# First loads, first modulation and x's split in one block; half of an output projection's operand split inside the attention; a context's sums shared out anew

## The reference, cut to what matters

```python
mod = (silu_c @ w_ada[l] + b_ada[l])[:, None, :]        # for x;   mod_c the same for the context
q, k, v, g_a, xb, b_g, c_g, g_b = split_cols(modulate(x, shift, scale) @ w_in, widths)
hc = modulate(xc, shift_c, scale_c)                     # through the same w_in
o_a = window_attention(q, k, v, kc, vc, sink)
o_b = b_g * short_conv(c_g * xb, conv_w)
y = jnp.concatenate([o_a * silu(g_a), o_b * silu(g_b)], axis=-1) @ w_out
x_new = layer_norm(DEEPNORM_ALPHA * x + gate * y, ln_g, ln_b)
```

## Time and profile before

| | us |
|---|---|
| median of three runs (2543.55 to 2545.18) | 2544.41 |
| the profiled execution | 2544.61 |
| its span, first to last instruction | 2542.8 |
| TensorE busy | 2305.4 (91%) |
| VectorE busy | 1462.5 (58%) |
| ScalarE busy | 1079.4 (42%) |
| GpSimd busy | 284.4 (11%) |
| mean granted TensorE clock, share of full | 0.954 |

### The profile page before, as it was taken

One profiled execution on the slowest core, in us unless ns is written; L12 is line 12 of the kernel. 1 busy time (PEld: TensorE's weight loads), 2 busy tenths in 40 slices (PEclk: granted clock), 3 DMA queues, 4 the chain that ended last, 5 costly groups with the idle time before them and its releaser, 6 DMA issues. The chain is left out here.

```text
span 2542.8 us, 35881 instructions
## 1 busy us (share of the span) xinstructions
PE 2305.4 (91%) x15162; PEld 1884.8 (74%) x15162; DVE 1462.5 (58%) x2187; ACT 1079.4 (42%) x1705; POOL 284.4 (11%) x156
## 2 busy tenths in 40 slices
PE   4999989789999969798889999998998889999996
PEld 2888766678888856576578888876776588888865
DVE  2233484648787773546677666345456677666354
ACT  2211373447658553334634334243335534333342
POOL 0100002513223210101011000011101010000011
PEclk7999899889999989899999999999999989999998
DMA  8111104311112112230022222312230012222311
GB/s 324 64 67 61 40 2 184 115 56 54 52 51 59 51 35 105 76 123 34 5 91 84 99 100 100 108 67 83 95 122 18 18 67 86 97 100 99 108 61 72
DMA packets 35104, 205.18 MB, mean 81 GB/s; under 512 B 3840, under 2 KB 5376, under 8 KB 14720
## 3 DMA queue, kind: packets, MB, share of 16 engines
q1 hardware_dynamic: 34944, 202.88, 22.8%
HBM read 200.77 MB, written 2.10 MB: 80 GB/s over the span
## 5 line engine op out<-in xcount | busy, mean ns | idle before, releaser
L309 PE MATMUL ps<-a_high,w_high 128*128 128x512 f32 (+1 forms) x1680 | 632.7, 377 | 35.5 <-DVE a_low L2405 22.7
L310 PE MATMUL ps<-a_low,w_high 128*128 128x512 f32 (+1 forms) x1680 | 621.8, 370 | 0.0
L311 PE MATMUL ps<-a_high,w_low 128*128 128x512 f32 (+1 forms) x1680 | 621.1, 370 | 0.0
L309 PEld LDWEIGHTS ps<-a_high,w_high 128*128 128x128 f32 x1680 | 320.8, 191 | 100.3 <-DVE w_low L2019 19.6
L2019 DVE TENSOR_TENSOR w_low<-raw_ring,w_high 128x2048 fp32r<-128x2048 f32 x102 | 233.8, 2292 | 270.6 <-ACT w_high L2013 265.9
L310 PEld LDWEIGHTS ps<-a_low,w_high 128*128 128x128 f32 x1680 | 321.4, 191 | 54.1 <-issue 2.5
L311 PEld LDWEIGHTS ps<-a_high,w_low 128*128 128x128 f32 x1680 | 321.2, 191 | 53.0
L2013 ACT ACTIVATE w_high<-raw_ring 128x2048 fp32r<-128x2048 f32 x102 | 195.2, 1914 | 367.0 <-PE ps L311 280.7
L309 PE MATMUL ps<-x_high,place_high 128*128 128x512 f32 (+1 forms) x720 | 261.5, 363 | 33.8 <-POOL x_low L325 25.4
L310 PE MATMUL ps<-x_low,place_high 128*128 128x512 f32 (+1 forms) x720 | 255.8, 355 | 0.0
L311 PE MATMUL ps<-x_high,place_low 128*128 128x512 f32 (+1 forms) x720 | 255.4, 355 | 0.0
(11 more groups left out here) (368 smaller groups left out, 3971.1 us busy)
## 6 DMA issues: line engine op xcount, KB each, us to landing
raw_ring<-w_dram SPq DMA_DIRECT2D x112, 1024.0 KB, 4.9
place_raw<-wc_dram SPq DMA_DIRECT2D x48, 512.0 KB, 3.6
ada_ring<-w_dram SPq DMA_DIRECT2D x12, 1024.0 KB, 17.0
arena<-w_dram SPq DMA_DIRECT2D x12, 1024.0 KB, 7.0
place_raw<-w_dram SPq DMA_DIRECT2D x11, 1024.0 KB, 4.9
ab_raw<-w_dram SPq DMA_DIRECT2D x10, 1024.0 KB, 5.0
x<-xT_dram SPq DMA_DIRECT2D x1, 2048.0 KB, 24.1
out_dram<-x SPq DMA_DIRECT2D x1, 2048.0 KB, 7.2
```

Of the source, the lines that this page charges most:

```text
L309: nc.tensor.matmul(out, wh, xh, start=start, stop=False)
L310: nc.tensor.matmul(out, wh, xl, start=False, stop=False)
L311: return nc.tensor.matmul(out, wl, xh, start=False, stop=stop)
```

## The change

- One block, `stage_start`, takes the place of the first three stages and of the split in `stage_ab_in`. The `w_ada` ring has 5 slots in the memory of later stages. SP's order is: 8 units, ab's unit 0, x and the context in four parts of two tiles each, 4 units, ab's unit 1. Once shift and scale are there (8 units), VectorE splits ab's unit 0, then modulates tile after tile and makes all lows; ScalarE makes the highs and then multiplies `X` by alpha, with the copies of rows 4 and 5 in between. The gate's part of the modulation is added at the block's end.
- `cb` is loaded in `stage_ab_in` and cast there at the third tile. GpSimd is no longer used for `SplitTiles`; VectorE makes all lows, in `stage_out1` too.
- In the attention, ScalarE makes the highs of tiles 4 to 7 of the output projection's operand before its first exponentials, and GpSimd their lows. `stage_mid` splits tiles 0 to 3 only, and its products go 4 to 7, 0 to 3.
- In the context's layer norm VectorE makes the last two of the seven adds of the sum, and adds the squares in pairs, so that four products take the place of eight. GpSimd makes its eight lows of x in a row. Of the context's modulation, ScalarE makes the even tiles and VectorE the odd ones.

```diff
-            def split_low(self, eng, which, k):
-                if k >= 0 and k % 2 == which:
-                    eng.wait_ge(self.S.rms_high, k + 1)
-                    (nc.vector if which else nc.gpsimd).tensor_tensor(
-                        self.low[k], self.src[k], self.high[k].bitcast(f32), O.subtract)\
-                        .then_inc(self.S.rms_odd if which else self.S.rms_even, 1)
+            def split_low(self, dve, k):
+                dve.wait_ge(self.S.rms_high, k + 1)
+                nc.vector.tensor_tensor(self.low[k], self.src[k], self.high[k].bitcast(f32), O.subtract)\
+                    .then_inc(self.S.operand, 1)
...
+        raw_cb = arena1[:, ab_mark:ab_mark + NCB]
...
+        def stage_start():
...
+            chunks = [slice(2 * i, 2 * i + 2) for i in range(4)]
+            tiles_in = SplitTiles(S, [yin[:, k, :] for k in range(KT)], xh, xl)
+            with nc.Block() as block:
+                @block.sync
+                def _(sp):
+                    def unit(u):
+                        if u >= 5:
+                            sp.wait_ge(S.used, u - 4)
+                        sp.dma_start(ring[u % 5], d["w1"][U0["ada0"] + u]).then_inc(arrived[u % 5], 16)
+                    sp.sem_clear(N.range)
+                    sp.sem_clear(w_range)
+                    sp.dma_start(v1[:, :], d["v1"]).then_inc(S.load, 16)
+                    sp.dma_start(cf[:, :], d["cf"]).then_inc(S.load2, 16)
+                    for u in range(8):
+                        unit(u)
+                    ab_stream.fetch(sp, src_ab, 0)
+                    for i, ks in enumerate(chunks):
+                        sp.dma_start(X[:, ks, 0:L], d["xT"][:, ks, :]).then_inc(x_arrived[i], 16)
+                        sp.dma_start(X[:, ks, L:T], d["ctxT"][:, ks, :]).then_inc(x_arrived[i], 16)
+                    for u in range(8, 12):
+                        unit(u)
+                    ab_stream.fetch(sp, src_ab, 1)
+                    sp.wait_ge(S.load, 16)
+                    sp.wait_ge(S.load2, 16)
+                @block.tensor
+                def _(pe):
+                    def flip(b):
+                        pe.wait_ge(S.act_out, b + 1)
+                        for j in range(4):
+                            last = nc.tensor.matmul(PS[:, 6 + b // 4, 8 * b + 2 * j:8 * b + 2 * j + 2],
+                                                    rows[b % 2][:, j * P:(j + 1) * P], picks_, start=True, stop=True)
+                        last.then_inc(S.flipped, 1)
+                    for u in range(12):
+                        pe.wait_ge(arrived[u % 5], 16 * (u // 5 + 1))
+                        if u == 0:
+                            pe.wait_ge(S.act_step, 1)
+                        w = ring[u % 5].rearrange("p (k n) -> p k n", k=KT)
+                        for k in range(KT):
+                            g = slice(32 * (k % 4), 32 * (k % 4) + 32)
+                            last = nc.tensor.matmul(PS[g, u // 2, (u % 2) * 256:(u % 2 + 1) * 256],
+                                                    cond_[:, k, :], w[:, k, :], start=(k < 4), stop=(k >= 4))
+                        last.then_inc(S.used, 1)
+                        if u == 2:
+                            pe.wait_ge(S.ready, 2)
+                        if u % 2 == 0 and 2 <= u < 8:
+                            flip(u // 2 - 1)
+                        if u == 7:
+                            flip(3)
+                    flip(4)
+                    flip(5)
+                @block.scalar
+                def _(act):
+                    def turn(b):
+                        act.wait_ge(S.used, 2 * b + 2)
+                        if b >= 2:
+                            act.wait_ge(S.flipped, b - 1)
+                        nc.scalar.activation(rows[b % 2], PS[:, b, :], A.Copy).then_inc(S.act_out, 1)
+                    act.wait_ge(S.load, 16)
+                    act.wait_ge(S.ready, 1)
+                    nc.scalar.activation(cond_[:, :, 0:2], v1[:, 0:16].rearrange("p (w k) -> p k w", w=2), A.Silu)\
+                        .then_inc(S.act_step, 1)
+                    for b in range(4):
+                        turn(b)
+                    ab_stream.split_high(act, 0)
+                    for k in range(KT):
+                        act.wait_ge(S.dve_out, 2 * k + 2)
+                        tiles_in.split_high(act, k)
+                        if k == 5:
+                            turn(4)
+                    for k in range(KT):
+                        nc.scalar.mul(X[:, k, :], X[:, k, :], ALPHA)
+                        if k == 3:
+                            turn(5)
+                @block.vector
...
+                    def modulation(parts, bank, b):
+                        v = slice(16 * parts[0], 16 * parts[-1] + 16)
+                        bias = v1[:, V1["b_ada0"][0] + 8 * parts[0]:V1["b_ada0"][0] + 8 * parts[-1] + 8]
+                        dve.wait_ge(S.flipped, b)
+                        link(nc.vector.tensor_tensor(mod[:, v].rearrange("p (j w) -> p j w", w=2),
+                                                     PS[:, bank, v].rearrange("p (j w) -> p j w", w=2),
+                                                     bias.unsqueeze(2).to_broadcast([P, 8 * len(parts), 2]), O.add))
+                    nc.vector.memset(padded_, 0.0).then_inc(S.ready, 1)
+                    dve.wait_ge(S.load2, 16)
+                    nc.vector.tensor_reduce(picks_, ident.rearrange("p (g x) -> p x g", g=4)[:, 0:2, :], AX, O.add)\
+                        .then_inc(S.ready, 1)
+                    dve.wait_ge(S.load, 16)
+                    modulation((0, 1), 6, 4)
+                    link(nc.vector.tensor_scalar(mod[:, 16:32], mod[:, 16:32], 1.0, None, O.add))
+                    ab_stream.split_low(dve, 0)
+                    for k in range(KT + 1):
+                        if k < KT:
+                            if k % 2 == 0:
+                                dve.wait_ge(x_arrived[k // 2], 32)
+                            for who, (a, b) in enumerate(((0, L), (L, T))):
+                                nc.vector.tensor_scalar(yin[:, k, a:b], X[:, k, a:b], modv(0, 1, who, k),
+                                                        modv(0, 0, who, k), O.mult, O.add).then_inc(S.dve_out, 1)
+                        if k:
+                            tiles_in.split_low(dve, k - 1)
+                    modulation((2,), 7, 6)
...
                     sp.sem_clear(N.range)
+                    ab_stream.load(sp, src_ab, RAW, RAW + 1)
                     sp.dma_start(ca, d["ca"]).then_inc(S.load, 16)
                     sp.dma_start(nsink, d["sink"]).then_inc(S.load, 16)
-                    ab_stream.load(sp, src_ab, RAW, 13 + RAW + 1)
+                    sp.dma_start(raw_cb, d["cb"]).then_inc(S.load2, 16)
+                    ab_stream.load(sp, src_ab, RAW + 1, 13 + RAW + 1)
                     sp.wait_ge(S.load, 32)
...
-                    ab_stream.split_high(act, u0)
-                    tiles_in.on_act(act)
...
-                    ab_stream.split_low(dve, u0)
-                    tiles_in.on_dve(dve)
-                    dve.wait_ge(S.load, 32)
                     for i, (kind, j) in enumerate(tiles):
                         if weight_tile.get((kind, j), 1) % 2 == 0:
                             ab_stream.split_low(dve, u0 + weight_tile[(kind, j)] // 2 + 1)
+                        if i == 2:
+                            dve.wait_ge(S.load2, 16)
+                            link(nc.vector.tensor_copy(cb[:, :], raw_cb))
+                            dve.wait_ge(S.load, 32)
...
+                    for k in range(NT4, KT):
+                        nc.scalar.activation(xh[k], yin[:, k, :], A.Copy).then_inc(S.rms_high, 1)
...
+                @block.gpsimd
+                def _(pool):
+                    for k in range(NT4, KT):
+                        pool.wait_ge(S.rms_high, k - NT4 + 1)
+                        nc.gpsimd.tensor_tensor(xl[k], yin[:, k, :], xh[k].bitcast(f32), O.subtract)
...
-            tiles_in = SplitTiles(S, [yin[:, k, :] for k in range(KT)], xh, xl)
+            tiles_in = SplitTiles(S, [yin[:, k, :] for k in range(NT4)], xh, xl)
+            ORDER = [4, 5, 6, 7, 0, 1, 2, 3]
...
                         gather(1, k)
                     pool.wait_ge(S.pe_tile, KT)
-                    for k in range(4):
-                        low(0, k)
-                    for k in range(6, KT):
-                        gather(1, k)
-                    for k in range(4, KT):
+                    for k in range(KT):
                         low(0, k)
                     for n in range(2):
...
-                            if i == 0:
+                        for k in ORDER:
+                            if i == 0 and k < NT4:
                                 tiles_in.tile(pe, k)
                             last = product3(bank(i), wh[:, k, :], wl[:, k, :], xh[k][:, ts], xl[k][:, ts],
```

(56 more changed lines are left out.)

176 lines of the change are left out of this document (28 added, 148 removed).

## The result

The changed kernel took 2530.05 us, median of five runs (2526.62 to 2535.06), against 2543.55 (2542.57 to 2545.18, five runs) for the kernel before on the same chip: ratio 0.9942, 95% interval 0.9931 to 0.9953, or 13.5 us less. The prediction was 2526.4 with a range of 2519.5 to 2533, so it holds, with the median 3.6 us above the point. A second set of five runs, on another chip, gave 2528.05 against 2543.37; the median of all ten runs is 2529.05.

The account below looks back on a forecast made before the run. TensorE is busy for 91% of the span, so time is won only where it waits or runs at half clock. 11.4 - 1.9 + 6.3 + 1.6 + 0.6 = 18.0 off 2544.6, less 0.2: 2526.4 us; range 2519.5 to 2533.

Parts of the forecast that it names:

- The start: First block up to the first tile's end: TensorE starts at 53.8, tile ends at 61.1 against 72.51, 11.4 us won.
- The attention: Highs and lows added ahead of the first exponentials: these come 1.45 late, 1.9 us lost if VectorE's first shift is caught.
- the two cases that the prediction drew from that page: Attention, VectorE beside GpSimd's lows: held by the port, 1.9 us lost; or no contention with one SBUF input, 1.45.
- The output projection's first tile: Products go 4 to 7, then 0 to 3, without a wait: ends at 396.9 against 403.15, 6.3 us won.
- The context's sums: Context's layer norm: mean at 485.5 instead of 488.6, root 1.0 earlier, later stretch 0.6 shorter; together 1.6 us won.
- the chain of four adds of squares: Context's norm: four VectorE adds, each behind a GpSimd low of 1.24, the fourth behind a unit split of 2.33; done 496.8.
- the modulation's chain: Context's norm after the reciprocal: VectorE's 20 short steps become 16, four of them on ScalarE; stretch 0.6 us shorter.
- The second output projection: All eight lows on VectorE, the first ready at about 955.5 rather than 956.1: 0.6 us won.
- (1): Context's sums: GpSimd gets no turn between VectorE's adds; gain there 6.5 instead of 1.6, total 2521.5; chance 0.16.
- (2): Attention pays for each low on VectorE, 5.0 instead of 1.9, and start's paths come 2 us late: 2531.5; chance 0.19.
- (3): First projection stays at half clock, 4.8 us more a tile, so the change is slower: 2555 at six tiles; chance 0.03.
- (4): Gain is absorbed because weight loads paced the first stages: about 2544; chance 0.04, with the change doing less than said.

Follow-up runs that it names:

- mod_again: Changed kernel with the context's modulation as before (VectorE modulates all eight tiles, ScalarE makes only highs), measured a second time: 2528.15 us, ratio 0.9942.
- start_alone: Kernel before with only the new first block (loads, first modulation, x's split): 2534.01 us, ratio 0.9963.
- attn_undone: Changed kernel with all eight tiles split in the output projection, none in the attention, lows on VectorE: 2528.68 us, ratio 0.9939.
- number 4: The experiment with attn_undone: changed kernel without the attention's splits, 2528.68 us, ratio 0.9939.
- Number 6: Changed kernel with the context's modulation as before, all eight tiles on VectorE, measured twice: 2527.24 us (ratio 0.9935) and 2528.15 us (0.9942).
- number 2: The experiment with start_alone: kernel before with only the new first block, 2534.01 us, ratio 0.9963.
- numbers 7 and 8: Changed kernel with GpSimd's eight lows waiting for the context's sum (2531.08 us, ratio 0.9953), or for the sums of squares (2536.21 us, 0.9963).
- after_again: The changed kernel measured again without any edit, against the kernel before: 2528.05 us, ratio 0.9943.

## Why the prediction was right, point by point

**The start: right, 12.3 won for 11.4.** First product at 53.4 for 53.8, tile done at 60.24 for 61.1; ScalarE ended at 53.07 and the gate's add behind the flips at 51.57 in this profile, at 54.20 and 53.41 in mod_again: within one to two microseconds of each other, the forecast having 53.5 and 53.2. Of the 0.9 left over, half is the earlier start and half that six products and not nine ran cold. The other nine profiles with this start had the tile done at 60.3 to 62.2, so 11.4 lies in the middle of them.

**The attention: the head right, the last 0.4 by luck.** The delay at the head was 1.53 for 1.45. The forecast made 1.9 of it by a VectorE step caught on the path, and that step failed. VectorE was caught, in an add of 128x12 that took 1.52 and ended at 292.53, where GpSimd's third low ended (292.50), and in the second unit's shift of 0.60, which ended with the second low; the first shift took 0.25 for 0.17. But ScalarE was behind with its highs and its table load until 290.58, so the catches held nothing: in VectorE's maxima of the 24 units (24, not the 20 given ahead), the changed kernel ran 1.5 behind the one before from the fifth to the twenty-second. The other 0.4 came in the last two, and there start_alone and attn_undone, which have no split in the attention, lost 0.4 as well. Against those two the splits cost 2.0 in this profile. Against the kernel before, the nine profiles with the splits lost 1.1 to 1.9 where the end ran at full clock and 3.1 to 3.5 where half clock fell on it (number 4). The Trainium skill's page "SBUF — State Buffer" (Who interferes with whom) gives the port to whichever started first, for its whole instruction; the add of two SBUF inputs agrees. Of the two cases that the prediction drew from that page for a step with one SBUF input, the 0.60 against 0.17 is the held one. Reductions that read PSUM took 1.21 and 1.22, as before (1.23), caught by nothing.

**The output projection's first tile: right, 6.33 for 6.3.** It starts at 380.89, without a wait for an operand and at full clock. Number 4 shares it out: 2.9 from VectorE making every low, 3.4 from the four operands that lie ready. Against the attention's loss the second is a gain of 1.5 to 2.3, as long as no half-clock stretch takes it.

**The context's sums: right sign, both terms mis-sized, and much of the gain hangs on the clock.** The mean came 3.5 earlier for 3.1. The root came 4.3 earlier for 1.0: the step that failed is the chain of four adds of squares, of which I put the first behind a low and the fourth behind a unit split of 2.33. The first add took 0.44 with no wait; the other three took 1.48 to 1.49, each one low, 1.41 apart and not 1.66, and the last of GpSimd's eight lows (10.81 in all, to 476.16) was the one that the fourth met. The other failed step is the modulation's chain, 0.6 won by forecast and 1.8 lost in fact (14.54 from the reciprocal to the next layer for 12.76). Counting VectorE's steps was wrong: three of its four lows now wait 0.62 for a high, and ScalarE has a modulation and two highs in each pair. Number 6 takes 1.0 of it back; the rest is the norms' 1.88 for 1.1, the first of them held by GpSimd's unit splits that run to 480.96. The sum, 3.53 + 0.76 - 1.78 = 2.5, lay above the 1.6 since the errors partly cancel. The forecast also took the eight variance products' 6.03 as the old order's price, but that was a half-clock price: at full clock the old order gets 1.9 of the 2.5 without any edit (number 2), and the new one is then only 0.6 ahead of it.

**The second output projection: right, 0.62 for 0.6.**

**The rivals.** (1) fell: the adds took turns, and numbers 7 and 8 show that without a low in flight they take 0.42 but that the tail gets longer, not shorter. In neither of the two was its gain to be had, since the port's work is only deferred. (2): the attention cost 1.9 in this profile and up to 3.5 in others (after_again: 95.6 from first scores to last mix, for 92.1), by the clock and not by catches, and never 5.0, and the start's paths were at most 0.7 us late (mod_again). (3): the first six products ran at 0.43 and the rest at 0.23, as at the dense start before, where nine did. (4): the 12.3 of the start stood undiminished at the attention, 12.26.

**What the sum missed.** The named parts come to 12.3 - 1.9 + 6.3 + 2.5 + 0.6 = 19.8, and 18.0 arrived. The median gain is 13.5 to 15.3: the forecast of 18.0 was 2.7 to 4.5 us too high, and the time lies in the range because the range was wide enough for the rivals. The step that was too sure is the one that took whatever is won at a mark to arrive at the end: in the unchanged part single profiles differ by up to 8 us. Against the 18.0 of the two profiles, the median is 3.4 us above the fastest run of the changed kernel, which was the profiled one, and the profiled run of before was one of its slower ones.

## What to carry to other kernels

Work taken off a port that two engines share is not saved by having one of them wait: look where the deferred work falls, and measure each place. Counting the steps of the busiest engine is no price for a chain of high, low and product that goes back and forth between two engines; follow one element through it. What a stretch gains should be held against the old stretch at the same clock: the old sums gained 1.9 us here by the clock alone. And where a few microseconds in 2500 are in question, compare the marks of several profiles, because the unchanged part varies by more.

## What the runs showed of the hardware

- A VectorE step on two SBUF inputs ended just behind the GpSimd low in flight, however small it was: 1.52 us for one of 128x12, and 1.49 for one of 128x256 that takes 0.42 alone. Even a tensor_scalar of 128x4 went from 0.17 to 0.60.
- VectorE's adds of squares took turns with GpSimd, one low to an add, and each slowed the other: three adds of 1.48 to 1.49 for 0.42 alone, beside lows of 1.45 for 1.28 alone.
- The table load of 1.28 us comes ahead of the first exponential, behind the four copies, and the exponential starts 0.02 us behind it.
- The same eight products of 256 columns for the variance took 6.03 us in one profile and 3.72 in another, at granted clocks of 0.61 and 1.00.
- At the attention's end, 24 products (eight transposes and sixteen mixes) took 3.7 us at a granted clock of 0.50 and 2.1 at 1.00.
- An unchanged stretch of some 2030 us took 2027.6 to 2035.5.
